# Rotary scores of block 1 in the mixer: one stacked product per head in place of a shared wide one

## The reference, cut to what matters

```python
q = jnp.concatenate([q[..., :QK_NOPE], rope(q[..., QK_NOPE:], positions)], axis=-1)
k_rot = rope(k_pe, positions)
k = jnp.concatenate([k_nope, jnp.broadcast_to(k_rot[:, :, None, :], (B, S, H, QK_ROPE))], axis=-1)
s = jnp.einsum('bqhd,bkhd->bhqk', qb, k) * scale
```

## Time and profile before

| | us |
|---|---|
| median of the three executions shown | 1083.3 |
| the profiled execution, its own time | 1084.16 |
| span of the profiled execution, first to last instruction | 1082.4 |
| TensorE busy | 1071.2 |
| VectorE busy | 869.5 |
| ScalarE busy | 530.2 |

### The profile page before, as it was taken

The page is one execution under the profiler, slowest core; times in us unless marked ns, Lnnn a source line. Parts: engine busy times, 40 slices in busy tenths (PEclk is TensorE's granted clock), DMA queues, the critical chain, the costliest instruction groups (busy, mean ns, idle before and its releaser), DMA issues.

```text
span 1082.4 us, 16425 instructions
## 1 busy us (share of the span) xinstructions
PE 1071.2 (99%) x5558; PEld 921.8 (85%) x5558; DVE 869.5 (80%) x1520; ACT 530.2 (49%) x731; POOL 84.6 (8%) x141
## 2 busy tenths in 40 slices
PE   8999999999999999999999999999999999999997
PEld 7888888999998888888888888889999988888885
DVE  6988777897855898878688887878988668987885
ACT  6544443656544644444455444445565545444442
POOL 0015001220000000000000000001300000000000
PEclk9999999999999999999999999999999999999999
DMA  9876675455564486666567666654455654866641
GB/s 321 285 225 191 208 229 154 133 155 190 170 223 150 139 257 211 192 204 189 159 182 247 204 191 194 197 157 134 154 174 163 222 166 137 266 190 203 185 144 39
DMA packets 156466, 203.96 MB, mean 188 GB/s; under 512 B 12960, under 2 KB 136096, under 8 KB 156416
## 3 DMA queue, kind: packets, MB, share of 16 engines
q1 hardware_dynamic: 152112, 192.55, 56.6%
q0 software_dynamic: 3488, 9.97, 3.4%
q10 hardware_dynamic: 816, 0.79, 0.2%
HBM read 202.22 MB, written 1.05 MB: 188 GB/s over the span
## 4 chain that ended last, share of the span: by engine, by line
PE 97%; DVE 2%; DMA 1%; issue 0%; POOL 0%; ACT 0%; DVEq 0%; POOLq 0%; ACTq 0%
PE ps L620 94%; PE ps L703 1%; DMA raw<-in_ffn_w 1%; DVE w_lo L1468 0%; PE ps L1108 0%; PE ps L874 0%; DVE xT L1481 0%; PE ps L961 0%; PE ps L1014 0%; DVE tmp L1716 0%; DVE x L1623 0%; PE ps L1069 0%; DVE tmp L1715 0%; DVE x L1599 0%; PE ps L1071 0%
## 5 line engine op out<-in xcount | busy, mean ns | idle before, releaser
L1468 DVE TENSOR_TENSOR w_lo<-raw,w_hi 128x1024 fp32r<-128x1024 f32 (+3 forms) x246 | 297.2, 1220 | 47.0 <-ACT w_hi L1202 44.8
L1202 ACT CAST w_hi<-raw 128x1024 fp32r<-128x1024 f32 (+3 forms) x246 | 252.8, 1044 | 161.7 <-PE ps L620 150.9
L620 PE MATMUL ps<-w_hi,xT 128*128 128x512 f32 (+1 forms) x912 | 286.9, 389 | 1.8 <-ACT w_hi L1194 1.8
L620 PEld LDWEIGHTS ps<-w_hi,xT 128*128 128x128 f32 x912 | 170.9, 188 | 37.8 <-issue 3.3
L1537 DVE STREAM_TRANSPOSE hidden_T<-ev 32x128 f32<-32x128 f32 x624 | 189.0, 303 | 11.2
L620 PE MATMUL ps<-w_hi,mixT 128*128 128x512 f32 x688 | 197.6, 390 | 0.0
L620 PE MATMUL ps<-v_flat,xT 128*128 128x512 f32 (+1 forms) x660 | 177.0, 389 | 0.0
L620 PE MATMUL ps<-w_lo,xT 128*128 128x512 f32 (+1 forms) x456 | 175.2, 388 | 0.0
L1202 ACT CAST v_flat<-raw 128x1024 fp32r<-128x1024 f32 (+1 forms) x114 | 118.2, 1045 | 85.2 <-PE ps L620 83.5
L620 PEld LDWEIGHTS ps<-w_hi,mixT 128*128 128x128 f32 x688 | 128.6, 188 | 26.3
L620 PEld LDWEIGHTS ps<-v_flat,xT 128*128 128x128 f32 x660 | 123.8, 188 | 25.4 <-DVE cqp L1468 0.2
(11 more groups left out here) (188 smaller groups left out, 1251.9 us busy)
## 6 DMA issues: line engine op xcount, KB each, us to landing
raw<-in_ffn_w SPq DMA_DIRECT2D x350, 256.0 KB, 3.5
raw<-in_ffn_w SPq DMA_DIRECT2D x88, 512.0 KB, 4.1
raw<-in_mem_wkv SPq DMA_DIRECT2D x32, 512.0 KB, 4.4
raw<-in_w_out SPq DMA_DIRECT2D x16, 512.0 KB, 5.1
raw<-in_mem_wq SPq DMA_DIRECT2D x16, 512.0 KB, 4.5
raw<-in_mem_wo SPq DMA_DIRECT2D x16, 512.0 KB, 6.4
gb<-in_ln_g POOLq DMA_DIRECT2D x16, 256.0 KB, 5.4
gb<-in_ln_b POOLq DMA_DIRECT2D x16, 256.0 KB, 4.8
```

Source lines behind the costliest of these rows:

```text
L620: return nc.tensor.matmul(dst, stand, move, start=start, stop=stop, skip_group_check=True)
L1202: nc.scalar.copy(slot_hi[slot[n]][:, 0:size], raw[:, n % RAW, 0:size]).then_inc(hi_done, 1)
L1468: nc.vector.tensor_tensor(slot_lo[slot[n]][:, s], raw[:, n % RAW, s], slot_hi[slot[n]][:, s].bitcast(F32), ALU.subtract).then_inc(lo_done, 1)
```

## The change

Keys: a new tile `keys_twice` (`mixT[:, 4, 0, :]`) holds the rounded rotary key on both halves of the partitions. ScalarE writes it with one full copy per block of tokens; the two half copies into `krT`'s rounded part are issued for block 0 alone. The remainders are written as before, with `keys_twice` as what is subtracted.

Queries of block 1: slot e of `qT[:, 6:9]` now belongs to head e. Its rounded query lies on its own half of the partitions and its remainder on the other half. ScalarE does this with two half copies in place of one full copy, VectorE with two half subtractions, each of which reads one half and writes the other. Block 0 stays as it was.

Scores of block 1: per head one product of the stacked query with `keys_twice`, and one with the remainder of `krT`, 256 columns each, in place of three products of 512 columns for both heads. Block 0's are issued as before.

```diff
+        keys_twice = mixT[:, 4, 0, :]
...
                 for dst, tokens, keys in ((s1, slice(P, S), slice(0, S)), (s0, slice(0, P), slice(0, P))):
-                    split_product(dst, (q[:, 0, tokens], q[:, 1, tokens]), (krT[:, :, 0, keys], krT[:, :, 1, keys]),
-                                  True, False)
+                    if dst is s0:
+                        split_product(dst, (q[:, 0, tokens], q[:, 1, tokens]), (krT[:, :, 0, keys], krT[:, :, 1, keys]),
+                                      True, False)
                     for e in range(2):
+                        if dst is s1:
+                            product(dst[:, e, :], q[:, e, tokens], keys_twice, e == 0, False)
+                            product(dst[:, e, :], q[:, e, tokens], krT[:, e, 1, :], False, False)
...
                     nc.scalar.copy(cq[:, :, 0, tokens], tiles(bank(m)[:, 0:384], 3))
-                    for e in range(2):
+                    last = nc.scalar.copy(keys_twice[:, tokens], bank(m)[:, 384:512])
+                    for e in range(2 if b == 0 else 0):
                         part = slice(e * QK_ROPE, (e + 1) * QK_ROPE)
                         last = nc.scalar.copy(krT[part, e, 0, tokens], bank(m)[part, 384:512])
...
-                    nc.scalar.copy(qT[:, 6:9, 0, b * P:(b + 1) * P], tiles(bank(m)[:, 0:384], 3)).then_inc(rope_hi, 1)
+                    if b == 0:
+                        nc.scalar.copy(qT[:, 6:9, 0, 0:P], tiles(bank(m)[:, 0:384], 3)).then_inc(rope_hi, 1)
+                        continue
+                    for e in range(2):
+                        part = slice(e * QK_ROPE, (e + 1) * QK_ROPE)
+                        last = nc.scalar.copy(qT[part, 6:9, e, P:S], tiles(bank(m)[part, 0:384], 3))
+                    last.then_inc(rope_hi, 1)
...
-                                                   krT[part, e, 0, tokens].bitcast(F32), ALU.subtract)
+                                                   keys_twice[part, tokens].bitcast(F32), ALU.subtract)
...
-                    nc.vector.tensor_tensor(qT[:, 6:9, 1, tokens], tiles(bank(m)[:, 0:384], 3),
-                                            qT[:, 6:9, 0, tokens].bitcast(F32), ALU.subtract).then_inc(bank_free, 1)
+                    if b == 0:
+                        nc.vector.tensor_tensor(qT[:, 6:9, 1, tokens], tiles(bank(m)[:, 0:384], 3),
+                                                qT[:, 6:9, 0, tokens].bitcast(F32), ALU.subtract).then_inc(bank_free, 1)
+                        continue
+                    for e in range(2):
+                        part, other = (slice(h * QK_ROPE, (h + 1) * QK_ROPE) for h in (e, 1 - e))
+                        last = nc.vector.tensor_tensor(qT[other, 6:9, e, tokens], tiles(bank(m)[part, 0:384], 3),
+                                                       qT[part, 6:9, e, tokens].bitcast(F32), ALU.subtract)
+                    last.then_inc(bank_free, 1)
```

## The result

| | median, us | runs |
|---|---|---|
| before, beside it on the same chips | 1083.42 | 22 |
| changed | 1084.96 | 22 |

The ratio is 1.0014, with a 95% interval of 1.0008 to 1.0020: 1.5 us slower (0.9 to 2.2), where +0.8 was forecast. The difference is 0.14% of the time, and the interval reaches up to the 0.2% that the prediction took as the least a measurement can tell.

What follows compares the result with a forecast made beforehand. The prediction put the chain of waits on TensorE for 97%, held in places by VectorE. Delays of 0.56 us in layer 0 and 0.30 in layer 1 made +0.86 on 1083.3, forecasting 1084.1 us, range 1082.5 to 1085.2.

Steps and rivals of the forecast that it cites:

- TensorE's saving, 0.21 a pair: Scores: four 256-column products replace three of 512, 0.56 against 0.77 us; 1.3 us over three pairs in two layers.
- Half subtractions at a whole one's duration, nothing overlapping: VectorE, block 1's turned queries: each half subtraction takes a whole one's 0.54 us, and the two run without overlap.
- slower: the crossing halves: Rival: VectorE instructions reading one half of the partitions and writing the other run slower; doubled gives 1086.3 us; chance 0.06.
- The bound from below, full overlap: Lower bound for VectorE's half subtractions: 0.465 us for both; layer 0 0.37 late, layer 1 about 0.1, +0.5 us.
- The instruction behind them 0.77 later: VectorE: the instruction behind the two half subtractions starts at 233.53 in place of 232.76, 0.77 us later.
- The handover of 0.15: Release of a bank from VectorE to TensorE: 0.15 us from a subtraction's end to the waiting item's start.
- the zero margin: Item 3 of v, layer 0: uqB's bank ready at 234.42 against TensorE's own 234.43, so no more delay.
- "About 0.5 us smaller" without the rule on held instructions: Without VectorE's hold when operands start on other partitions, the delay would be 0.465 and the sum about 0.5 us smaller.
- The savings vanish at the turning of pair 0 and at its values: TensorE waits there for VectorE's chain from the pooling product; the three scores' savings vanish and the 0.56 us delay stays.
- Layer 1's keys, 0.27 ahead: Block 1's one key copy puts VectorE 0.27 us ahead; in layer 1 this lasts, so that layer ends 0.3 late.
- Covers: ScalarE's extra copies cost nothing: block 0's key copy (about 0.17 us) and query copies (about 0.5) finish before VectorE wants them.
- The rival in which the saving arrives: Rival: TensorE bounds throughout, so its saving counts: 1082.0 us, or 1081.7 with layer 1's 0.27; chance 0.09.

Runs made afterwards that it cites:

- scores_only: Changed kernel with block 1's query copies and subtractions whole, as before (its rotary scores not right); median 0.29 us below before.
- queries_only: Kernel before with only block 1's queries laid out by half copies and crossing subtractions, old products and keys; median 1.77 us above before.
- after_split_later: Changed kernel with VectorE's third weight split moved from ahead of pair 0's maxima to behind its probabilities; median 0.45 us above before.
- after_both: Changed kernel with the pooling product between items 1 and 2 of v and the third weight split behind pair 0's probabilities; median 1.35 us below before.

## Why the prediction was right, and where it was short

- **TensorE's saving, 0.21 a pair**: 0.20 in score 2. Right.
- **Half subtractions at a whole one's duration, nothing overlapping**: 0.55 each, where 0.54 was taken. The crossing of the halves costs at most 0.01, so the rival "slower: the crossing halves" is out. The bound from below, full overlap, too.
- **The instruction behind them 0.77 later, and uqB's subtraction with it**: here the sum was short. The copy was held as I took it (0.81 later), but uqB's subtraction was held as well, so that it came 0.92 later. Item 3 of v, for which I had found exactly no further wait, waits once more and pays its start behind a wait again. The pooling product was 0.73 late in layer 0, not 0.56.
- **The handover of 0.15** from the end of VectorE's instruction to TensorE's start, read off item 0 of v: the halves end at 232.61 and item 2 starts at 232.66, so it was 0.05 there, and 0.06 at item 3 (233.50 to 233.56). Only at the values of pair 0 was it 0.14 (247.72 to 247.86). So item 2 came 0.40 late and not 0.48, which by luck hid a part of what item 3 added, whose wait made the pooling product 0.2 later still. With the halves swapped, where uqB's subtraction comes only 0.81 later, the pooling product is still 0.61 late (26.75 against 26.14): of the 0.73 the second hold is 0.11 to 0.12, and the rest of what exceeds 0.56 comes from item 3's wait, which the zero margin had left out.
- **"About 0.5 us smaller" without the rule on held instructions**: a slip. By the prediction's own lower bound (0.37 and 0.1) the sum would be about 0.4 smaller.
- **The savings vanish at the turning of pair 0 and at its values**: shown by scores_only (nothing gained), queries_only (nothing more lost) and after_split_later (gained back when the chain is shortened). The 0.73 of the pooling product is 0.69 at the end of the stage.
- **Layer 1's keys, 0.27 ahead**: 0.23 at TensorE's wait and 0.27 to 0.29 by the single changes. Layer 1 came out 0.46 late, not 0.30, again by the hold of uqB's subtraction.
- **Covers**: ScalarE's extra copies cost nothing to be seen, in block 0's keys as in the queries.
- **The tail of 0.23** was in no part of the sum.

The mechanism stands; the sum was +0.86 and came out at 1.38 in the traces and 1.54 in the medians (0.9 to 2.2). The mis-sized term is the delay of uqB's subtraction, 0.92 us where 0.77 was taken (0.15 a layer short, 0.10 of it by the second hold, as the order of the halves shows), which a zero margin at item 3 of v passed on; the tail of 0.23 was left out.

The rival in which the saving arrives needed TensorE free at two places. It wasn't, but two moves of other work make it so, and then the saving is there: after_both.

## What to carry to other kernels

A matmul stream without an idle row can still be held: look for a pitch a few hundredths too long and for a release that ends just ahead of a start. Savings in front of such a place go into the wait, delays pass through, and the fix is to shorten the chain that ends there (here one weight split moved, and a product moved into the wait). Count a VectorE instruction on other partitions than its neighbours not by its duration alone, but with the overlap that it and up to two instructions behind it lose; and where a margin comes out at exactly zero, put an error of a tenth on it.

## What the runs showed of the hardware that I had not expected

- A VectorE instruction loses its overlap also by one that stands two places ahead: 0.44 in place of 0.33 us from copy to subtraction, restored to 0.34 by the order of the halves.
- Two more VectorE instructions in the program, at either of two places, moved the end of the execution by 0.23 us. The cause is open.
- Two executions of nearly the same kernel differ by 1.6 us in their first wait for weights, and by 0.92 at the first transpose of the mixer, so that spans of single profiles can't be compared at this scale, while distances inside a stage repeat within a few hundredths.
